# GpSimd's sum jobs in the three cycles around the exchange of the resident operands

## The chip, the cores and the metric

The kernel runs on one core of one Trainium2 chip. The metric is the device time of one execution in microseconds (us), lower is better. TensorE (PE) multiplies, VectorE (DVE) and ScalarE (ACT) work on tiles in SBUF and PSUM, GpSimd (POOL) too, and DMAs move data between HBM and SBUF. DMAs are issued from three queues here: SyncE's (SP), ScalarE's and GpSimd's.

## The reference, cut to what matters

One layer: RMSNorm, a chunked spatial-gating mixer, a residual add, RMSNorm, a squared-ReLU MLP, a residual add and the final RMSNorm. The change lies in how the MLP is computed.

```python
def channel_mlp(h, w1, w2):
    a = jax.nn.relu(h @ w1)
    return (a * a) @ w2
# h: 2048 x 1024, w1: 1024 x 4096, w2: 4096 x 1024, float32
x = x + mixer_chunked_sgu(rmsnorm(x, norm_mix_g[i]), ...)
x = x + channel_mlp(rmsnorm(x, norm_mlp_g[i]), mlp_w1[i], mlp_w2[i])
return rmsnorm(x, final_g)
```

## The kernel before, in words

**Precision.** Every float32 operand of TensorE is split into a rounded part and a rest: ScalarE writes the `_hi` copy (`u_hi`, `x_hi`, `a_hi`, `d_hi`), VectorE subtracts it from the raw tile and writes `_lo`. Each product is three matmuls (hi x hi, hi x lo, lo x hi).

**Stages.** First the mixer, in four blocks of 512 tokens (`BLOCKS` = 4), until about 577 us. Then the MLP by a 2 x 2 block scheme that needs seven products where eight would be usual, but needs sums and differences of blocks as operands. The up stage (h times w1) has `UP` = 16 cycles of `STEPS` = 7 steps, `SECOND` = 112 steps in all; a step is 24 matmuls of 512 columns. The down stage (times w2) has 8 cycles of 7 steps of 48 matmuls. TensorE runs through both in order (line 1263).

**The resident operands.** In the up stage the seven token operands `x_raw[0..6]` of 1 MB each stay in SBUF for eight cycles (`UP // PAIRS` = 8), and the weights `u_raw` (512 KB a step, four slots) stream past them. Steps 0 to 55 work on the first pair of token blocks, steps 56 to 111 on the second. The exchange is written out by hand. When step 49 + i has ended, operand i is free, and ScalarE's queue issues the load of its successor (`up_operand(act, 1, i)`, line 302). ScalarE and VectorE split it in step 52 + i (`renew`, lines 581 and 849), and TensorE needs it in step 56 + i. So the loads of 7 MB are issued from the end of step 49 on, and the splits go on to step 58.

**The order on each engine.** Instructions of an engine run in the order of the program. In step g, ScalarE and VectorE first split the weight of step g + 2 (`ahead`: lines 571 and 838), then take or finish results, then split a resident operand (`renew`). ScalarE copies products out of the PSUM banks (`keep_bank`, line 755); step g needs the banks of step g - 2. VectorE makes the operands of the down stage from the results (`finish_second`, lines 1017 to 1029), in two halves, in the third and fourth step of the next cycle. ScalarE's copy in that fourth step overwrites what `finish_second` reads, and so waits for it.

**GpSimd's jobs.** The weight sums are made by `add_up(n)`, 40 jobs in the order of `jobs`. A job waits until the job before it is stored, loads 1 MB into the one tile `job`, makes four dependent 128 x 512 `tensor_tensor` operations on it (lines 491 to 497, both inputs in SBUF), and stores 1 MB (`w1sum`, `xs` or `w2sum`, line 507). Twenty jobs are done in the mixer stage. In the up stage `next_jobs` is called once a cycle, after `pool.wait_ge(products, step_done(u * STEPS))`, which is the end of the first step of cycle u: two jobs in cycles 0 and 1, one in each later cycle, but none in cycles 6, 7 and 8. What is left is done in the down stage, after four accumulating DMAs onto `Y` (line 542). The sums `w2sum` of chunk 2 are needed before the 17th step of the down stage and those of chunk 3 before its 24th.

Counted from the code: jobs 24 to 27 run in cycles 2 to 5, jobs 28 to 34 in cycles 9 to 15, jobs 35 to 39 in the down stage.

Of the kernel before, what the change touches and what calls it, by code (L numbers as in the profile page):

```python
# [31 lines left out]
def build(nc: bass.Bass, x, xT, gains_T, final_g, a_w_in, a_w_s, a_b_s, a_w_out,  # L32
          mlp_w1, mlp_w2, out):
    _, L, D = x.shape
    F = mlp_w2.shape[1]
    G = a_w_s.shape[1]
# [4 lines left out]
    PAIRS = BLOCKS // 2  # L41
# [10 lines left out]
    UP = PAIRS * CHUNKS * 2  # L52
# [106 lines left out]
    with ExitStack() as ctx:  # L159
# [78 lines left out]
        def step_done(g, j=None):  # L238

            j = width(g) - 1 if j is None else j  # L240
            return 4 * FIRST + (2 * g if g < SECOND else 4 * g - 2 * SECOND) + j + 1
# [210 lines left out]
        def _(pool):  # L452
# [63 lines left out]
            def next_jobs(count):  # L516
                nonlocal n
                for _ in range(count):
                    if n < len(jobs):
                        add_up(n)  # L520
                        n += 1
# [8 lines left out]

            for u in range(UP):
                pool.wait_ge(products, step_done(u * STEPS))
                if not UP // PAIRS - 2 <= u <= UP // PAIRS:
                    next_jobs(2 if u < 2 else 1)


            for half, cols, i in FIRST_PARTS:
# [767 lines left out]
```

## Time and profile before

| what | value |
|---|---|
| time, median of 3 runs | 1824.14 us (1823.81 to 1824.42) |
| the profiled execution | 1827.29 us |
| span of the profile (first to last instruction) | 1825.5 us |
| granted TensorE clock, mean | 0.996 |
| busy: TensorE, VectorE, ScalarE, GpSimd | 1802.2, 1111.1, 782.5, 407.1 us |
| moved by DMA | 445.40 MB, mean 244 GB/s |

The span is given from the first instruction, and all positions in the trace count from there. A busy TensorE is one with matmuls in flight; "idle before" is the time in which an engine had none, with what ended it. The granted clock 1.00 is 2.4 GHz and 0.50 is 1.2 GHz.

### The profile page before, as it was taken

The page shows a single profiled execution, that of the slowest core. Times are in us where ns is not written, and L with a number is a line of the kernel's source. Part 1 is how long each engine was busy: PE and PEld are TensorE (multiplying, and loading weights), DVE is VectorE, ACT ScalarE, POOL GpSimd, SP SyncE. Part 2 cuts the span into 40 slices and gives each one's busy share as a digit, 9 for nine tenths or more (in the row PEclk, how much of TensorE's full clock was granted, in tenths as well). Part 3 has the DMA queues.
Part 4 walks back from the last instruction along what each step waited for, and adds up shares of the span by engine and source line. Part 5 has one row for each costly group of instructions (what it writes and reads, how often), then busy time and mean ns, then how long its engine had stood idle before and what let it go on. Part 6 is the DMA issues. An engine that isn't in the chain of part 4 may idle for free.

```text
span 1825.5 us, 20165 instructions
## 1 busy us (share of the span) xinstructions
PE 1802.2 (99%) x8136; PEld 1497.9 (82%) x8136; DVE 1111.1 (61%) x1122; ACT 782.5 (43%) x880; POOL 407.1 (22%) x394
## 2 busy tenths in 40 slices
PE   9999999999999899999999999999999999999998
PEld 7888888888888788888878888878888888888886
DVE  3583483484384566654666655685666666866665
ACT  5553544434534533444543443354433335333333
POOL 2442442432340133310002111110234002000002
PEclk9999999999999899999999999999999999999999
DMA  8757656665655588875957777799977555854552
GB/s 329 269 209 267 240 215 241 244 244 204 234 199 201 199 290 267 303 263 183 355 197 237 259 256 229 278 367 319 309 299 264 220 202 201 288 184 185 199 205 103
DMA packets 134157, 445.40 MB, mean 244 GB/s; under 512 B 8112, under 2 KB 9136, under 8 KB 118320
## 3 DMA queue, kind: packets, MB, share of 16 engines
q1 hardware_dynamic: 105728, 329.02, 51.3%
q0 software_dynamic: 25168, 92.80, 14.3%
q10 hardware_dynamic: 3168, 22.30, 3.2%
q8 instruction: 64, 1.05, 0.2%
q14 instruction: 29, 0.24, 0.0%
HBM read 318.26 MB, written 125.83 MB: 243 GB/s over the span
## 4 chain that ended last, share of the span: by engine, by line
PE 92%; DVE 2%; DMA 2%; ACT 1%; SPq 1%; issue 1%; DVEq 0%; POOLq 0%; POOL 0%; ACTq 0%
PE bank L1263 62%; PE bank L1098 28%; DMA u_raw<-in_mlp_w 1%; PE bank L1144 1%; PE bank L1120 1%; SPq L312 1%; DMA bias_rows<-in_a_b_s 1%; PE bank L1147 0%; DMA x_raw<-xs 0%; DVE Y L1036 0%; ACT x_hi L581 0%; DVE x_lo L849 0%; DVE r L1017 0%; DVE sums L1020 0%; DVE u_lo L838 0%
## 5 line engine op out<-in xcount | busy, mean ns | idle before, releaser
L1263 PE MATMUL bank<-x_hi,u_hi 128*128 128x512 f32 x896 | 351.0, 392 | 8.0 <-ACT c L755 4.8
L1263 PE MATMUL bank<-x_lo,u_hi 128*128 128x512 f32 x896 | 349.9, 391 | 0.0
L1263 PE MATMUL bank<-x_hi,u_lo 128*128 128x512 f32 x896 | 349.8, 390 | 0.0
L1263 PE MATMUL bank<-d_lo,a_hi 128*128 128x512 f32 x896 | 348.9, 389 | 0.0
L1263 PE MATMUL bank<-d_hi,a_hi 128*128 128x512 f32 x896 | 348.9, 389 | 0.0
L1263 PE MATMUL bank<-d_hi,a_lo 128*128 128x512 f32 x896 | 348.9, 389 | 0.0
L838 DVE TENSOR_TENSOR u_lo<-u_raw,u_hi 128x1024 fp32r<-128x1024 f32 x112 | 148.9, 1329 | 180.2 <-ACT u_hi L571 180.2
L1007 DVE TENSOR_TENSOR Y<-bank,Y 128x512 f32<-128x512 f32 x208 | 138.0, 686 | 179.8 <-PE bank L1263 179.6
L576 ACT ACTIVATE d_hi<-d_raw 128x2048 fp32r<-128x2048 f32 x56 | 107.4, 1919 | 282.2 <-DMA d_raw<-w2sum 153.7
L832 DVE TENSOR_TENSOR w_lo<-w_raw,w_hi 128x2048 fp32r<-128x2048 f32 x47 | 116.5, 2490 | 171.5 <-ACT w_hi L566 160.5
L1263 PEld LDWEIGHTS bank<-x_hi,u_hi 128*128 128x128 f32 x896 | 168.9, 189 | 45.6 <-issue 8.4
L1263 PEld LDWEIGHTS bank<-x_hi,u_lo 128*128 128x128 f32 x896 | 168.9, 189 | 35.3
L1263 PEld LDWEIGHTS bank<-x_lo,u_hi 128*128 128x128 f32 x896 | 169.0, 189 | 34.6
L1263 PEld LDWEIGHTS bank<-d_hi,a_lo 128*128 128x128 f32 x896 | 168.3, 188 | 34.8
L1263 PEld LDWEIGHTS bank<-d_hi,a_hi 128*128 128x128 f32 x896 | 168.3, 188 | 34.8
L1263 PEld LDWEIGHTS bank<-d_lo,a_hi 128*128 128x128 f32 x896 | 168.3, 188 | 34.8
L571 ACT ACTIVATE u_hi<-u_raw 128x1024 fp32r<-128x1024 f32 x112 | 117.1, 1057 | 136.9 <-DMA u_raw<-in_mlp_w 63.4
L755 ACT ACTIVATE c<-bank 128x512 f32<-128x512 f32 x96 | 55.5, 596 | 216.7 <-DVE sums L1029 112.2
L844 DVE TENSOR_TENSOR d_lo<-d_raw,d_hi 128x2048 fp32r<-128x2048 f32 x56 | 128.9, 2302 | 23.1 <-ACT d_hi L576 23.1
L855 DVE TENSOR_TENSOR a_lo<-a_raw,a_hi 128x2048 fp32r<-128x2048 f32 x56 | 132.3, 2363 | 6.2 <-ACT a_hi L585 6.2
L585 ACT ACTIVATE a_hi<-a_raw 128x2048 fp32r<-128x2048 f32 x56 | 107.4, 1917 | 49.8 <-DMA a_raw<-a2s 49.8
L491 POOL TENSOR_TENSOR job<-job 128x512 f32<-128x512 f32 x32 | 55.6, 1737 | 240.3 <-DMA job<-in_mlp_w 240.3
(113 smaller groups left out, 2763.3 us busy)
## 6 DMA issues: line engine op xcount, KB each, us to landing
a_raw<-a2s SPq DMA_DIRECT2D x56, 1024.0 KB, 7.3
a2s<-sums SPq DMA_DIRECT2D x32, 1280.0 KB, 7.9
job<-in_mlp_w POOLq DMA_DIRECT2D x32, 1024.0 KB, 8.2
u_raw<-w1sum SPq DMA_DIRECT2D x64, 512.0 KB, 4.7
d_raw<-w2sum SPq DMA_DIRECT2D x32, 1024.0 KB, 4.9
w_raw<-in_a_w_in SPq DMA_DIRECT2D x31, 1024.0 KB, 5.9
u_raw<-in_mlp_w SPq DMA_DIRECT2D x48, 512.0 KB, 5.4
d_raw<-in_mlp_w SPq DMA_DIRECT2D x24, 1024.0 KB, 5.2
```

The costliest lines, as they stand in the source:

```text
L491: pool.tensor_tensor(q3, q3, q1, ALU.subtract).then_inc(job_step, 1)
L571: act.activation(u_hi[g % SLOTS][:, :, :], u_raw[g % SLOTS][:, :, :], ACT.Copy)\
L576: act.activation(d_hi[d % SLOTS][:, :, :], d_raw[d % SLOTS][:, :, :], ACT.Copy)\
L585: act.activation(a_hi[d % SLOTS][:, :, :], a_raw[d % SLOTS][:, :, :], ACT.Copy)\
L755: act.activation(to, bank_of(g, j)[:, :], func).then_inc(act_read, 1)
L832: dve.tensor_tensor(w_lo[s][:, :, :], w_raw[s][:, :, :], f32(w_hi[s][:, :, :]), ALU.subtract)\
L838: dve.tensor_tensor(u_lo[s][:, :, :], u_raw[s][:, :, :], f32(u_hi[s][:, :, :]), ALU.subtract)\
L844: dve.tensor_tensor(d_lo[s][:, :, :], d_raw[s][:, :, :], f32(d_hi[s][:, :, :]), ALU.subtract)\
L855: dve.tensor_tensor(a_lo[s][:, :, :], a_raw[s][:, :, :], f32(a_hi[s][:, :, :]), ALU.subtract)\
L1007: dve.tensor_tensor(rows, bank_of(g, j)[:, :], rows, ALU.add).then_inc(dve_read, 1)
L1098: ins = pe.matmul(banks[j][:, :], stationary(x_part, k, j), moving(y_part, k, j), start=first and k == 0 and n == 0, stop=final and k == K ...
L1263: ins = pe.matmul(bank_of(g, j)[:, :], stationary[x_part][:, k, j * P:(j + 1) * P], moving[y_part][:, k, :], start=i in (0, 1, 3) and k == ...
```

## The change

GpSimd calls `next_jobs` in every cycle of the up stage, in 6, 7 and 8 too. Nothing else is edited. Since the jobs are numbered through, job 28 runs in cycle 6, 29 in cycle 7, 30 in cycle 8, and each later cycle has the job that stood three cycles behind it. Cycle 15 ends with job 37, and jobs 38 and 39 stay for the down stage.

```diff
             for u in range(UP):
                 pool.wait_ge(products, step_done(u * STEPS))
-                if not UP // PAIRS - 2 <= u <= UP // PAIRS:
-                    next_jobs(2 if u < 2 else 1)
+                next_jobs(2 if u < 2 else 1)
```

## Rows read from the trace of the kernel before

**Rows 1.** The page: busy time by engine, and the chain's shares by engine.
```profile
PE 1802.2 (99%) x8136; PEld 1497.9 (82%) x8136; DVE 1111.1 (61%) x1122; ACT 782.5 (43%) x880; POOL 407.1 (22%) x394
...
PE 92%; DVE 2%; DMA 2%; ACT 1%; SPq 1%; issue 1%; DVEq 0%; POOLq 0%; POOL 0%; ACTq 0%
```

**Rows 2.** Windows: stretch, length, busy PE PEld DVE ACT POOL, clock, DMA share, GB/s.
```profile
787.00:825.00 38.00, 38.00 (x169) 31.50 (x168) 23.89 (x25) 15.47 (x23) 7.70 (x6) 1.00 0.73 250
825.00:863.00 38.00, 38.00 (x169) 31.47 (x169) 19.93 (x25) 15.70 (x23) 0.00 (x0) 1.00 0.61 193
863.00:901.00 38.00, 37.48 (x166) 30.77 (x165) 25.12 (x27) 16.76 (x19) 0.00 (x0) 1.00 0.92 331
901.00:939.00 38.00, 34.53 (x152) 27.99 (x151) 28.29 (x29) 24.05 (x32) 0.00 (x0) 1.00 0.63 212
...
1167.00:1205.00 38.00, 36.48 (x161) 29.62 (x160) 23.00 (x23) 16.41 (x20) 7.79 (x6) 1.00 0.93 347
...
1282.00:1358.00 76.00, 76.00 (x337) 62.96 (x337) 51.95 (x42) 30.81 (x20) 19.30 (x15) 1.00 0.86 305
```

**Rows 3.** Timeline of GpSimd: start, length, instruction, idle before and its end.
```profile
788.79 0.71 POOL L481 DMA_DIRECT2D job<-in_mlp_w  x1 [15.59 <-PE bank L1263]
...
946.29 0.71 POOL L481 DMA_DIRECT2D job<-in_mlp_w  x1 [141.35 <-PE bank L1263]
955.72 1.54 POOL L491 TENSOR_TENSOR job<-job 128x512 f32<-128x512 f32 x1 [8.71 <-DMA job<-in_mlp_w]
...
1174.39 0.71 POOL L481 DMA_DIRECT2D job<-in_mlp_w  x1 [21.94 <-PE bank L1263]
1186.16 1.29 POOL L491 TENSOR_TENSOR job<-job 128x512 f32<-128x512 f32 x1 [11.06 <-DMA job<-in_mlp_w]
...
1309.72 3.32 POOL L491 TENSOR_TENSOR job<-job 128x512 f32<-128x512 f32 x1 [21.72 <-DMA job<-in_mlp_w]
```

**Rows 4.** Timeline of ScalarE and its queue in the exchange.
```profile
864.75 0.33 ACTq L302 DMA_DIRECT2D x_raw<-xs  x1
...
879.05 1.06 ACT L571 ACTIVATE u_hi<-u_raw 128x1024 fp32r<-128x1024 f32 x1 [2.89 <-DMA u_raw<-in_mlp_w]
885.26 0.60 ACT L755 ACTIVATE c<-bank 128x512 f32<-128x512 f32 x1 [5.15 <-DVE sums L1029]
...
897.49 1.06 ACT L571 ACTIVATE u_hi<-u_raw 128x1024 fp32r<-128x1024 f32 x1 [3.84 <-DMA u_raw<-in_mlp_w]
...
928.28 1.08 ACT L755 ACTIVATE c<-bank 128x512 f32<-128x512 f32 x2 [10.16 <-DVE sums L1029]
```

**Rows 5.** Timeline of VectorE, in the exchange and in cycle 15.
```profile
905.51 2.29 DVE L849 TENSOR_TENSOR x_lo<-x_raw,x_hi 128x2048 fp32r<-128x2048 f32 x1 [4.83 <-ACT x_hi L581]
...
923.17 1.22 DVE L838 TENSOR_TENSOR u_lo<-u_raw,u_hi 128x1024 fp32r<-128x1024 f32 x1
...
927.55 0.69 DVE L1029 TENSOR_TENSOR sums<-sums 128x512 f32<-128x512 f32 x1
...
1187.73 2.18 DVE L838 TENSOR_TENSOR u_lo<-u_raw,u_hi 128x1024 fp32r<-128x1024 f32 x1 [2.41 <-ACT u_hi L571]
1189.83 1.77 DVE L1017 TENSOR_TENSOR r<-r 128x512 f32<-128x512 f32 x1
```

**Rows 6.** The chain that ended last, in order of time: start, length, what.
```profile
886.44 11.03 DMA u_raw<-in_mlp_w
...
929.02 250.52 PE bank L1263 x1104
```

**Rows 7.** Windows in the exchange, columns as in Rows 2.
```profile
878.00:892.00 14.00, 13.85 (x62) 11.13 (x60) 8.83 (x10) 7.80 (x8) 0.00 (x0) 1.00 0.99 353
892.00:906.00 14.00, 13.64 (x60) 11.36 (x61) 9.17 (x9) 10.16 (x14) 0.00 (x0) 1.00 1.02 373
```

**Rows 8.** Windows after a stop of TensorE of 4.4 us, and around one of 3.4 us.
```profile
616.00:622.00 6.00, 6.00 (x24) 5.18 (x24) 1.19 (x2) 3.48 (x5) 0.00 (x0) 0.67 0.50 201
920.00:935.00 15.00, 11.59 (x51) 9.31 (x50) 12.47 (x16) 4.33 (x6) 0.00 (x0) 1.00 0.45 158
```

## The prediction

> **What bounds the kernel now.** Read the page first: TensorE is busy 99% of the span and makes 92% of the chain that ended last [rows 1]. So a change off TensorE can gain only where TensorE stands idle, and costs only where it makes a new idle stretch. Next, look at each cycle in the windows. In an up cycle with a job (787 to 825 us) TensorE is busy 38.00 of 38.00 us, in one without (825 to 863) too [rows 2]. The idle time sits in the exchange: 38.00 - 37.48 = 0.5 us in cycle 7, then 38.00 - 34.53 = 3.5 us in cycle 8, and 38.00 - 36.48 = 1.5 us in cycle 15, where the down operands are loaded [rows 2]. The down stage, 1282 to 1358, shows 76.00 of 76.00 [rows 2].
>
> The third view is the chain in order of time, read backwards from TensorE's restart at 929.02 [rows 6]. ScalarE's bank copy at 928.28 had waited 10.16 us for VectorE's `sums` of line 1029, begun at 927.55 [rows 4, 5]. VectorE's 22 instructions from 905.51 to that point follow each other without a gap over 0.3 us, and before the first it had waited 4.83 us for ScalarE's `x_hi` [rows 5]. ScalarE in turn had waited 3.84 us until 897.49 for a weight, and that load was issued at 886.44 and took 11.03 us [rows 4, 6]. So the stop of 3.5 us has two parents: a weight that lands late in a stretch whose DMA share is 0.99 to 1.02 [rows 7], and then some 23 us of VectorE work without a pause. Neither contains a GpSimd job: it is idle for 141.35 us before 946.29 [rows 3]. The change puts jobs into both.
>
> **What moves.** Three jobs move from the down stage into cycles 6, 7 and 8; per job 1 MB is loaded, four operations are made, 1 MB is stored. The count of instructions is the same.
>
> Removed from the down stage: 3 MB of loads, 3 MB of stores, 12 GpSimd operations. I cost this at nothing, because TensorE had no idle time where they stood [rows 2]. Had that cover not been there, the most that these jobs take from VectorE would be the amount worked out below, about 4 us each. What comes next there is the accumulating DMAs and jobs 38 and 39, which now end earlier; jobs 31 to 37 run in the same slots as 28 to 34 did, with other addresses. Nothing is late that was in time.
>
> Added in cycle 6: the job's turn comes one cycle after the window that began at 788.79 plus 38, so near 827 us, and with 9.4 us from issue to the first operation, as from 946.29 to 955.72 [rows 3], some 7 us of operations and a store as long as the load it is over by about 853. DMA share is 0.61 there, against 0.73 with a job in the cycle before, and the exchange begins at 864.75 [rows 2, 4]. TensorE was fully busy in the same phase with a job. Cost 0.
>
> Added in cycle 7: GpSimd waits for step 49, the very step that frees the first operand, so its load is issued at about 865, together with the first of the seven operand loads [rows 4]. Cycle 15 is the twin of this moment: a job's load issued at 1174.39 next to the first operand loads of the down stage had its first operation 11.8 us after the issue, where 9.4 is seen in a quiet cycle [rows 3]. I take 12 us: the four operations stand at about 877 to 884. VectorE's chain there starts with the weight that landed at 879.05 and ends with `finish_second`, for which the bank copy at 885.26 waited [rows 4]. In the twin the same operations grew: 2.18 us where the split of a weight takes 1.22 without a job, and 1.77 where a short operation takes 0.69 [rows 5], about 1 us for each GpSimd operation met. Two or three are met, so 2 to 3 us; with 1 to 2 us for the weight itself (1 MB more at 353 GB/s is 3.0 us if it all stands ahead, 0 if none does [rows 7]) the bank copy comes 3 to 5 us later. TensorE needed that bank when step 53 ended, which is when the weight load of 886.44 was issued [rows 6], so a new stop of some 3.5 us appears at step 54. It does not add to the later one in full: ScalarE has 3.84 us of waiting at 893.65 to 897.49 and VectorE 4.83 us before 905.51 [rows 4, 5], and these take up a shift of up to about 4 us. TensorE loses the same time earlier, not twice.
>
> What does reach the end is the delay of the 886.44 load itself. The job's store, issued at about 884 to 885, runs beside it: 1 MB at 353 to 373 GB/s [rows 7] is 2.8 to 3.0 us. Bounds 0 (TensorE's new stop postpones the competing operand loads) and 3.0; a single load shared with one more stream is neither, so I take the middle, **1.4 us**.
>
> Added in cycle 8: GpSimd waits for step 56. It ended near 904 (946.29 is seven steps later: minus 38 minus 3.5 us of stop), in the new kernel near 907. First operation 9.4 us behind the issue [rows 3], all four at about 916 to 923, in the middle of VectorE's unbroken stretch that sets TensorE's restart. The price of four such operations beside dense VectorE work is a pair of rows: 23.89 us of VectorE time in a cycle with a job, 19.93 in one without, both with 25 instructions, so 3.96 us [rows 2]. In the twin, where VectorE had gaps, the three operations that met it grew by about 3.1 us (0.96 + 1.08 + 1.08, of which two rows stand) [rows 5]. The stretch here has no gap, so I take **3.9 us**; bounds 0 (the operations miss the stretch) and 4.4 (1.1 us each).
>
> For this I weigh a rule. The rows show a VectorE operation with both inputs in SBUF growing by 1 us, not by GpSimd's whole 1.3 to 1.5 us [rows 2, 3, 5]. The Trainium skill (SBUF — State Buffer, section Who interferes with whom) says that such an operation and a GpSimd one that reads SBUF exclude each other for the whole instruction. By that rule, taken to the letter, 4 x 1.29 = 5.2 us would be lost, not 3.9, and the forecast would be 1.3 us later. It speaks against this change in either form; the trace agrees with the sign and puts the size lower.
>
> TensorE's clock: after a stop of 4.4 us it was granted 0.67 on average over 6 us, that is partly the 1.2 GHz level; around the 3.5 us stop it stayed at 1.00 [rows 8]. If a stop now reaches 4.4 us at the end, 6 x (1 - 0.67) = 2 us more are lost. Split into two stops, each may stay under; I take 0, bound 2.0.
>
> **Sum.** 0 + 0 + 1.4 + 3.9 + 0 = +5.3 us, against the profiled execution's own 1827.29: 1832.6. That execution lies 3.15 us above the median of the plain runs; on the median 1824.14 the same sum gives **1829.4 us**. The lowest sum with the VectorE term in the middle of the stretch is +3.1, the highest 3.0 + 4.4 + 2.0 = +9.4.
>
> **The rivals.** Measurement can tell about 0.2%, or 3.6 us.
>
> (a) Hidden, not slower: the cycle 8 job misses VectorE's stretch. It would have to land after 928, that is take 20 us and more; one load did wait 21.72 us, beside accumulating DMAs [rows 3]. Against it: those DMAs are absent, and the last operand load is issued after step 55, some 33 us behind 864.75 [rows 4]. Equally the waits of 3.84 and 4.83 us may take up more than I grant them. Then 0 to 3.0 us remain, 1824.1 to 1827.1, about 1825.5. The point from which it decides is whether GpSimd's operations start before about 925. Chance 0.20.
>
> (b) The loads pile up: the exchange is already at full DMA share for 28 us [rows 7], and load and store of the cycle 7 job both go ahead of the 886.44 weight: 2 x 3.0 + 3.9 + 2.0 for the clock = 11.9, so 1836. Against it: work that waits less urgently, the operands themselves, can give way. Chance 0.07.
>
> (c) Faster: the last sums leave the down stage, where one job waited 21.72 us for its load [rows 3]. If the slow loads there cost TensorE time, it would be gained. The windows show none [rows 2], so this is worth at most a fraction of a microsecond unless the plain runs differ from the profiled one; 1820 would need idle time that is not there. Chance 0.03.
>
> The forecast has 0.70. Of it about 0.06 lies under +3.6 us. So slower by over 0.2%: 0.64 + 0.07 = 0.71; within: 0.20 + 0.06 = 0.26; faster 0.03. The range runs from +1.1 (inside rival a) to +9.4: 1825.2 to 1833.5.
>
> **What would show it.** In the profile of the changed kernel: GpSimd operations at about 877 to 884 and 916 to 923; short VectorE operations of 1.7 us there instead of 0.69; a stop of TensorE before step 54 (near 887 to 890) and one before step 61 that ends near 934; the weight of 886.44 landing at 897.5 to 900.5; the down stage unchanged at full occupation. The forecast is wrong if VectorE has gaps between 907 and 930, if the cycle 8 operations start after 925, or if the weight lands far later than 900.5.

## The result

| | median, us | profiled execution, us |
|---|---|---|
| before | 1824.14 (1823.19 to 1824.42, 5 runs) | 1827.29 |
| changed | 1832.79 (1832.41 to 1832.91, 5 runs) | 1832.79 |

The ratio is 1.005, with a 95% interval of 1.0038 to 1.0061: the change costs 8.65 us by the medians, 7 to 11 by the interval. One of the ten executions of only8_late, a kernel of the experiments, took 5369 us for a reason that no trace shows, and is in no comparison.

The page of the changed kernel, as in [rows 1], and rows picked from two views, the chain in order of time and GpSimd's timeline (start, length, what):

```profile
PE 1803.2 (98%) x8136; PEld 1498.2 (82%) x8136; DVE 1113.0 (61%) x1122; ACT 782.5 (43%) x880; POOL 399.6 (22%) x394
...
PE 92%; DMA 3%; DVE 2%; SPq 1%; issue 1%; ACT 1%; DVEq 0%; POOLq 0%; POOL 0%
```
```profile
865.47 10.81 DMA u_raw<-in_mlp_w
884.40 12.78 PE bank L1262 x48
897.19 13.75 DMA u_raw<-w1sum
916.65 2.32 DVE u_lo L837
933.01 251.94 PE bank L1262 x1104
```
```profile
860.31 0.71 POOL L481 DMA_DIRECT2D job<-in_mlp_w  x1 [21.93 <-PE bank L1262]
873.57 1.28 POOL L491 TENSOR_TENSOR job<-job 128x512 f32<-128x512 f32 x1 [12.55 <-DMA job<-in_mlp_w]
...
902.91 0.71 POOL L481 DMA_DIRECT2D job<-in_mlp_w  x1 [22.06 <-PE bank L1262]
913.31 1.28 POOL L491 TENSOR_TENSOR job<-job 128x512 f32<-128x512 f32 x1 [9.69 <-DMA job<-in_mlp_w]
914.66 3.24 POOL L493 TENSOR_TENSOR job<-job 128x512 f32<-128x512 f32 x1
```

The shares of the page hardly move, so the windows have to be read. Columns are those of [rows 2]:

```profile
825.00:863.00 38.00, 38.00 (x169) 31.47 (x168) 23.81 (x26) 15.47 (x23) 7.78 (x6) 1.00 0.73 251
863.00:901.00 38.00, 35.36 (x149) 28.79 (x148) 24.88 (x26) 18.54 (x23) 6.74 (x5) 0.96 0.99 382
901.00:939.00 38.00, 29.64 (x124) 23.84 (x123) 29.91 (x27) 16.88 (x18) 9.73 (x6) 0.91 0.68 236
...
1282.00:1358.00 76.00, 76.00 (x337) 62.94 (x336) 48.95 (x39) 32.75 (x20) 17.03 (x14) 1.00 0.88 299
```

Cycle 6 with its job keeps TensorE fully busy, and so does the down stage. The idle time of the two windows of the exchange is 2.6 and 8.4 us, where it was 0.5 and 3.5 [rows 2], and matmuls are missing for a second reason: the clock's mean falls to 0.96 and 0.91. TensorE's restarts (idle before in brackets):

```profile
884.40 0.47 PE L1262 MATMUL bank<-x_hi,u_hi 128*128 128x512 f32 x1 [2.64 <-ACT c L754]
933.01 0.77 PE L1262 MATMUL bank<-x_hi,u_hi 128*128 128x512 f32 x1 [7.81 <-ACT c L754]
```

To compare kernels I count from the first operand load, which is issued when step 49 ends. In the changed kernel it is this row, against 864.75 before [rows 4]:

```profile
860.10 0.33 ACTq L302 DMA_DIRECT2D x_raw<-xs  x1
```

TensorE's restart before step 61 lies 933.01 - 860.10 = 72.9 us behind it; before it was 929.02 - 864.75 = 64.3 [rows 4, 6]. That is +8.6 us. Then the clock:

```profile
933.00:940.00 7.00, 6.99 (x25) 5.70 (x26) 4.16 (x5) 4.61 (x7) 0.00 (x0) 0.79 0.01 2
```

Behind the restart 7 us were granted 0.79 on average, part of them at 1.2 GHz, so 7 x 0.21 = 1.5 us of matmul time went, where the clock had stayed at 1.00 around the stop before [rows 8]. In these two profiled executions the exchange is thus 10.1 us longer. The medians differ by less, 8.65 us, probably because the clock can fall behind the unchanged stop too, as the experiments show (0.59 to 0.78); it did not in the execution shown ahead.

### The profile page after: what moved, and what is told of

Same layout as the page of the kernel before. It is cut to its first block, busy times and chain, and to the rows that moved or that the text cites. A ratio compares the mean times of both kernels' runs of the same rounds, so it can differ in the third digit from the quotient of the medians.

```text
span 1831.0 us, 20167 instructions
## 1 busy us (share of the span) xinstructions
PE 1803.2 (98%) x8136; PEld 1498.2 (82%) x8136; DVE 1113.0 (61%) x1122; ACT 782.5 (43%) x880; POOL 399.6 (22%) x394
## 4 chain that ended last, share of the span: by engine, by line
PE 92%; DMA 3%; DVE 2%; SPq 1%; issue 1%; ACT 1%; DVEq 0%; POOLq 0%; POOL 0%
PE bank L1262 62%; PE bank L1097 27%; PE bank L1143 1%; DMA u_raw<-in_mlp_w 1%; PE bank L1119 1%; DMA u_raw<-w1sum 1%; SPq L312 1%; DMA bias_rows<-in_a_b_s 1%; PE bank L1146 0%; DVE Y L1035 0%; DVE r L1016 0%; DMA x_raw<-xs 0%; DVE sums L1019 0%; DVE u_lo L837 0%; SPq L328 0%
## 5 line engine op out<-in xcount | busy, mean ns | idle before, releaser
L854 DVE TENSOR_TENSOR a_lo<-a_raw,a_hi 128x2048 fp32r<-128x2048 f32 x56 | 127.9, 2285 | 6.3 <-ACT a_hi L584 6.3
L565 ACT ACTIVATE w_hi<-w_raw 128x2048 fp32r<-128x2048 f32 x47 | 89.5, 1909 | 41.8 <-DMA w_raw<-in_a_w_out 21.7
```

Source lines behind the costliest of these rows:

```text
L565: act.activation(w_hi[w % SLOTS][:, :, :], w_raw[w % SLOTS][:, :, :], ACT.Copy)\
L854: dve.tensor_tensor(a_lo[s][:, :, :], a_raw[s][:, :, :], f32(a_hi[s][:, :, :]), ALU.subtract)\
```

## The experiments

All ratios are against runs of the kernel before on the same chip, with 95% intervals; 0.001 is 1.8 us. "Restart" is TensorE's restart before step 61, counted from the first operand load; "stop" its idle time there; "clock" the mean grant over the 7 us behind the restart, from windows like the one above. These three come from one profiled execution of each kernel. The ratios rest on 4 (ops_only) to 12 (writes_only) executions of the kernel named. The kernels dma_only, ops_only, ops8_only and writes_only leave out or alter some of the weight sums, so their results are wrong and only their times count.

| kernel | ratio | restart, us | stop, us | clock |
|---|---|---|---|---|
| before | 1 | 64.3 | 3.41 | 1.00 |
| changed | 1.0050 (1.0038 to 1.0061) | 72.9 | 7.81 | 0.79 |
| only6 | 1.0006 (0.9997 to 1.0016) | 66.4 | 3.41 | 0.59 |
| only7 | 1.0013 (1.0002 to 1.0025) | 67.9 | 3.7 | 0.76 |
| only8 | 1.0028 (1.0016 to 1.0040) | 67.3 | 6.59 | 0.60 |
| only8_late | 1.0006 (0.9996 to 1.0015) | 64.4 | 3.42 | 0.76 |
| dma_only | 1.0020 (1.0010 to 1.0030) | 67.6 | 3.98 | 0.76 |
| ops_only | 1.0051 (1.0036 to 1.0066) | 70.0 | 5.89 | 0.60 |
| ops8_only | 1.0036 (1.0023 to 1.0048) | 68.0 | 6.58 | 0.75 |
| writes_only | 1.0016 (1.0005 to 1.0027) | 63.4 | 3.41 | 0.78 |
| order_after | 1.0034 (1.0022 to 1.0047) | 70.3 | 5.99 | 0.61 |
| pause7_8_15 | 0.9988 (0.9979 to 0.9997) | 63.3 | 2.17 | 1.00 |
| order_before | 0.9979 (0.9971 to 0.9988) | 61.9 | 0.54 | 1.00 |
| order_pause | 0.9969 (0.9958 to 0.9979) | 60.8 | 0.92 | 1.00 |

### Which of the three jobs costs

```diff
-                next_jobs(2 if u < 2 else 1)
+                if u not in (7, 8):      # only6;  only7: (6, 8);  only8: (6, 7)
+                    next_jobs(2 if u < 2 else 1)
```

> Pause in cycles 7 and 8 only, so job 28 runs in cycle 6 and nothing runs in the exchange. Theory A (the price is paid where a job meets the exchange): same as the kernel before, +0.0, bounds -0.5 to +0.7 us; the stop before step 61 stays at about 3.5 us. Rival B (what costs is that jobs come earlier or that the down stage has fewer of them): a third of the loss, about +3 us.

Measured 1.0006, +1.1 us (-0.5 to 2.9), an interval that includes 1. The 3 us of rival B (a third of the loss for each) lie at its upper end. The cycle 6 job costs nothing that can be told.

The profile of only6 also shows how far single executions scatter. GpSimd is idle for 108 us before 946.33 there, and yet the restart is 2.1 us later than before: the weight load issued at 881.64 took 13.17 us, where its counterpart took 11.03 [rows 6], and TensorE stood idle for 2.43 us before 906.34. So a difference of some 2 us in the restart of two single executions proves nothing.

> Pause in cycles 6 and 8, so one job runs in cycle 7, beside the first operand loads. Theory A: a new stop of about 3 us before step 54, taken up again by ScalarE's and VectorE's waiting; at the end +1 to +3 us, through a weight that lands later. Rival C (two jobs are needed to make the queue of loads too long, one is absorbed): +0 to +0.7 us. Rival B: +3 us.

Measured 1.0013, +2.4 us (0.4 to 4.6), which excludes 0 narrowly, and does not by itself separate the rivals (C up to 0.7, B 3) from theory A. The new stop before step 54 is there, 2.52 us. From the chain of this kernel:

```profile
865.63 11.41 DMA u_raw<-in_mlp_w
...
884.43 12.80 PE bank L1263 x48
897.25 12.15 DMA u_raw<-w1sum
```

The weight that comes late is the one issued after step 55 (897.25, for step 59), not the one of step 53 on which the prediction looked.

> Pause in cycles 6 and 7, so one job runs in cycle 8, whose four operations fall into VectorE's unbroken stretch. Theory A: VectorE's operations there grow by 3.3 us and the stop before step 61 with them; with 0 to 2 us for its load and 1.4 us where TensorE's clock falls to 0.50 after the longer stop, +4 to +6 us. Rival C (the operations cost little, it is the loads): +0 to +2 us.

Measured 1.0028, +5.1 us (2.9 to 7.3), inside theory A's band, and rival C (0 to 2) falls. VectorE's timeline, columns as in [rows 5]:

```profile
913.95 2.32 DVE L838 TENSOR_TENSOR u_lo<-u_raw,u_hi 128x1024 fp32r<-128x1024 f32 x1
916.20 1.79 DVE L1017 TENSOR_TENSOR r<-r 128x512 f32<-128x512 f32 x1
917.91 1.77 DVE L1020 SCALAR_TENSOR_TENSOR sums<-c 128x512 f32<-128x512 f32 x1
919.60 1.77 DVE L1023 TENSOR_TENSOR sums<-sums,r 128x512 f32<-128x512 f32 x1
```

These four operations grew by about 1.1 us each; the next is back at 0.68. TensorE's stop went from 3.41 to 6.59 us:

```profile
931.40 0.77 PE L1263 MATMUL bank<-x_hi,u_hi 128*128 128x512 f32 x1 [6.59 <-ACT c L755]
```

### The same job five steps later

```diff
-                next_jobs(2 if u < 2 else 1)
+                if u == 8:
+                    pool.wait_ge(products, step_done(61))
+                if u not in (6, 7):
+                    next_jobs(2 if u < 2 else 1)
```

> Pause in cycles 6 and 7; the job of cycle 8 waits for the end of step 61 in place of step 56, so that it falls behind VectorE's stretch and the exchange. Theory A (it is the place that costs): same as before, 0 to +1 us, against +5.1 us for the same job five steps earlier. Rival B (a further job in the up stage costs wherever it stands): about +5 us.

Measured 1.0006, +1.1 us (-0.7 to 2.7), so rival B's 5 us fall; the stop is again 3.42 us. It is the place that costs, not the job.

### Transfers and operations apart

```diff
+                if n in (29, 30):        # dma_only: one column in place of 512
+                    for i in range(4):
+                        pool.tensor_tensor(job[:, i, 0:1], job[:, i, 0:1], job[:, i, 1:2], ALU.subtract)
+                        ...              # the semaphore steps as in the other jobs
```

> All three jobs at their places, but the jobs of cycles 7 and 8 make their four operations on one column only, so those 2 MB of sums hold other values: their transfers stay, their load on SBUF goes. Theory A (in the changed kernel the stretch from step 49 to step 63 is 10.1 us longer: 5.3 us by weights that land late, 3.3 by VectorE's operations grown beside GpSimd's, 1.4 by TensorE's clock): about +5 us against the kernel before, +4 to +6.5, with VectorE's short operations at 0.69 us throughout. Rival D (GpSimd's operations are nearly all of it): +0 to +2 us.

Measured 1.0020, +3.6 us (1.8 to 5.5), between theory A's band (4 to 6.5) and rival D's (0 to 2), and clear of zero: the transfers do cost. VectorE's short operations were 0.69 us, and the chain is that of only7: a load of 11.37 us issued at 865.99, a stop of 2.06 us before step 54, and the weight issued after step 55 (897.09) late again, with 12.44 us.

```diff
+                load(29)                 # in cycle 6; ops_only
+                for m, step in ((29, step_done(52, 0)), (30, step_done(58))):
+                    pool.wait_ge(products, step)
+                    ... the four operations of job m on the same tile
+                pool.wait_ge(products, step_done(62))
+                store(29); load(30); store(30)
```

> Three jobs, but of those of cycles 7 and 8 the load comes before the exchange, the operations of both stand in the middle of step 52 and after step 58, and the store, a load and a store come after step 62; the second set works on the first's data, so those sums hold other values. No job transfer lies in the exchange, the operations do. Theory A: +3.3 us by VectorE's growth before step 61, and up to 1.5 us more by the clock: +3 to +5 us. Rival E (the transfers are all of it, the growth is hidden): +0 to +1 us.

Measured 1.0051, +9.3 us (6.6 to 12.0): over both theories, and as much as the whole change, though only four executions stand behind it. The restart explains 70.0 - 64.3 = 5.7 of it, the clock 7 x 0.40 = 2.8 more. VectorE's timeline has both groups:

```profile
874.48 2.00 DVE L867 TENSOR_TENSOR u_lo<-u_raw,u_hi 128x1024 fp32r<-128x1024 f32 x1 [3.22 <-ACT u_hi L600]
876.41 1.78 DVE L1046 TENSOR_TENSOR r<-r 128x512 f32<-128x512 f32 x1
878.11 1.78 DVE L1049 SCALAR_TENSOR_TENSOR sums<-c 128x512 f32<-128x512 f32 x1
...
912.82 1.79 DVE L1046 TENSOR_TENSOR r<-r 128x512 f32<-128x512 f32 x1
914.54 1.78 DVE L1049 SCALAR_TENSOR_TENSOR sums<-c 128x512 f32<-128x512 f32 x1
916.24 1.77 DVE L1052 TENSOR_TENSOR sums<-sums,r 128x512 f32<-128x512 f32 x1
917.94 1.78 DVE L1054 TENSOR_TENSOR sums<-r,sums 128x512 f32<-128x512 f32 x1
```

The second group adds 4 x 1.09 = 4.4 us to the stretch that sets the restart. The first adds 3 us early, of which 1.3 to 1.4 seem left at 5.7 - 4.4; that is within the scatter of single executions seen in only6. Theory A had left out such a carry, and put the clock too low. A further 0.76 us is a stop before 1008.98, outside the exchange: the jobs displaced behind step 62 come in quick succession there, and the four operations of one, from 998.37 on, meet VectorE's next `finish_second`. To separate the groups, the first was moved behind step 58 and the second behind step 62:

```diff
-                for m, step in ((29, step_done(52, 0)), (30, step_done(58))):
+                for m, step in ((29, step_done(58)), (30, step_done(62))):
```

> As ops_only, but the first set of four operations stands after step 58 and the second after step 62, behind the exchange: no job transfer in the exchange and one set in VectorE's stretch. Revised theory F (ops_only restarted TensorE 5.8 us later than the kernel before: 4.4 by the four short operations grown in the stretch, 1.4 carried over from the stop before step 54; then 2.8 by the clock): the 1.4 go, so VectorE's second finish ends 4.4 us later and the kernel is 4.4 to 7.5 us slower than before. If the first set was the cause, under +2 us.

Measured 1.0036, +6.6 us (4.2 to 8.8), inside the expected band; under 2 us, as for the first set as the cause, is excluded. Four operations in the stretch and no job transfer near it give about what job 30 alone gave (only8, 5.1): the cycle 8 job costs by its operations. The two intervals (2.9 to 7.3 and 4.2 to 8.8) overlap, so its transfer may still be worth up to about 3 us.

### What of GpSimd's work blocks VectorE

```diff
-                        pool.tensor_tensor(to, a, b, ALU.add if i == 2 else ALU.subtract).then_inc(job_step, 1)
+                        pool.memset(job[:, :, :], float(i)).then_inc(job_step, 1)
```

> ops_only with each operation replaced by a memset of the whole tile, so GpSimd writes SBUF and reads none of it; those sums hold constants. Theory F with the shared read interface as the cause: VectorE's operations stay at 0.69 us, the stop before step 61 is that of the kernel before, and the time is +0 to +1.5 us (the jobs displaced into the later cycles stay displaced). Rival G (any GpSimd work on SBUF blocks VectorE): growth by about 1 us an operation as in ops_only, +8 to +9 us.

GpSimd was as busy at the same places, but VectorE's operations did not grow there:

```profile
909.24 7.44 POOL L542 MEMSET job<- 128x2048 f32 x4 [28.14 <-PE bank L1292]
```
```profile
911.50 0.69 DVE L1046 TENSOR_TENSOR r<-r 128x512 f32<-128x512 f32 x1
912.10 0.69 DVE L1049 SCALAR_TENSOR_TENSOR sums<-c 128x512 f32<-128x512 f32 x1
912.70 0.69 DVE L1052 TENSOR_TENSOR sums<-sums,r 128x512 f32<-128x512 f32 x1
```

The stop is 3.41 us again, and rival G falls. The time, +2.9 us (0.9 to 4.9), is above the expected 0 to 1.5. The profile shows two parts of it: the clock behind the stop (7 x 0.22 = 1.5 us), and a stop of 0.72 us before 1002.00 like that of ops_only. There a displaced job's `tensor_tensor` operations, from 991.00 on, met VectorE's `finish_second`, and three VectorE operations grew by 1.1 us each. No run tests these displaced jobs alone. Against ops_only, which differs only in the eight operations themselves (the memsets also write the whole tile each), it is about 6 us faster. The Trainium skill (SBUF — State Buffer, section Who interferes with whom) says that a VectorE instruction with two SBUF inputs contends with a GpSimd one that reads SBUF and not with one that only writes; these two runs agree, 1.78 us against 0.69.

### Which work on VectorE sets the restart, and a faster kernel

In step 58 VectorE splits the last operand, which TensorE needs only in step 62, ahead of the second half of `finish_second`, for which the restart waits. The edit exchanges the two:

```diff
                 if c and i in (2, 3):
                     finish_second(c - 1, i - 2)
-                renew(g)
+                second = UP // PAIRS * STEPS
+                if g == second + 3:
+                    renew(g - 1)
+                if g != second + 2:
+                    renew(g)
```

> The changed kernel, with the split of the last operand moved behind finish_second's second half on VectorE. If VectorE's stretch sets the restart in the changed kernel, as in the one before: 2.3 us faster than the changed kernel and up to 1.5 more by the clock, so +4.5 to +6.5 us against the kernel before. If the late weight alone sets it, +8.6 us.

Measured 1.0034, +6.2 us (4.0 to 8.6), so 2.9 us better than the changed kernel by the two central ratios, inside the expected band; the two intervals overlap, though, and the 8.6 us of the rival are the end of this one. The restart is 2.6 us earlier. The clock gave part of it back: 0.61 in place of 0.79.

> The kernel before, with that one move and its own pause in cycles 6, 7 and 8. The same kernel with the pause in 7, 8 and 15 ran 5.6 us faster than before, of which the pause alone gave 2.2: so 3.4 us faster, -2.3 to -4.

The kernel that this expectation quotes is order_pause, which ran before it and stands below. Measured 0.9979, -3.8 us (-5.3 to -2.2); the stop shrinks from 3.41 to 0.54 us, with the clock at 1.00.

> Pause in cycles 7, 8 and 15, a job in every other cycle, so that cycle 15, where the down operands are loaded, has none either. By theory A the stop of 1.5 us in cycle 15 belongs to VectorE's operations grown by 3.1 us beside the job of that cycle: it goes, and the kernel is 1 to 1.5 us faster than before. By the rival that the stop is the down operands' own, 0.

Measured 0.9988, -2.2 us (-3.8 to -0.5), so the rival's 0 lies just outside. In cycle 15 the stop of 1.5 us [rows 2] is gone. Of this kernel, columns of [rows 2]:

```profile
1167.00:1205.00 38.00, 38.00 (x169) 31.49 (x168) 23.24 (x27) 19.61 (x24) 0.00 (x0) 1.00 0.90 314
```

> The kernel with the pause in cycles 7, 8 and 15, and on VectorE the split of the last operand (2.28 us) moved from before finish_second's second half to behind it. If VectorE's stretch sets the stop before step 61, that stop gets 2.2 us shorter and the kernel is about 4 us faster than before (2.2 us of which the pause alone gave). If something else ends last there, no more than the pause's 2.2 us.

Measured 0.9969, -5.7 us (-7.7 to -3.8): within the intervals, the two gains add up. This kernel is faster than both, and it does the opposite of the change: it widens the pause by cycle 15, and only cycle 6 is taken out of it.

## Why the prediction was right, and where it was not

**Right.** The sign and the range (1825.2 to 1833.5 against 1832.79). Cycle 6 costs nothing that can be told (only6). The jobs removed from the down stage bring 0: its windows are full in both. The first stop appears before step 54, at 884.40, 2.64 us where some 3.5 were expected. VectorE's stretch sets the restart and GpSimd's operations stand in it, from 913.31 on; that is 53.2 us behind the first operand load, where the expected 916 is 51.3. Rival (a), hidden, failed at its own point: the operations started well before 925. Rival (c) found no idle time to win.

**The VectorE term, 3.9 us.** In the changed kernel four operations met the stretch and three grew in full:

```profile
914.40 2.33 DVE L848 TENSOR_TENSOR x_lo<-x_raw,x_hi 128x2048 fp32r<-128x2048 f32 x1
916.65 2.32 DVE L837 TENSOR_TENSOR u_lo<-u_raw,u_hi 128x1024 fp32r<-128x1024 f32 x1
918.90 1.77 DVE L1016 TENSOR_TENSOR r<-r 128x512 f32<-128x512 f32 x1
920.60 1.78 DVE L1019 SCALAR_TENSOR_TENSOR sums<-c 128x512 f32<-128x512 f32 x1
```

1.10 + 1.08 + 1.09 = 3.3 us. At the first of the four VectorE lost next to nothing (2.33 for 2.28); there it was GpSimd's operation of 914.66 that took 3.24 us, where most take 1.3 to 1.6. The mechanism and the bounds held. In only8 and ops8_only it was 4.4. Neither came to the 5.2 us of mutual exclusion over whole instructions.

**The transfer term, 1.4 us: the failed step.** It was put on the weight issued at 886.44. In the changed kernel that load was issued at 881.79 and ScalarE split it at 892.16 without waiting. The late one was two steps on, the weight of step 59, and ScalarE did wait for it:

```profile
910.97 1.06 ACT L570 ACTIVATE u_hi<-u_raw 128x1024 fp32r<-128x1024 f32 x1 [4.97 <-DMA u_raw<-w1sum]
912.06 1.23 DVE L837 TENSOR_TENSOR u_lo<-u_raw,u_hi 128x1024 fp32r<-128x1024 f32 x1 [3.74 <-ACT u_hi L570]
```

The same weight before, its issue and VectorE's split of it:

```profile
898.09 5.76 SPq L337 DMA_DIRECT2D u_raw<-w1sum  x2
911.44 1.22 DVE L838 TENSOR_TENSOR u_lo<-u_raw,u_hi 128x1024 fp32r<-128x1024 f32 x1
```

VectorE's split began 912.06 - 860.10 = 52.0 us behind the first operand load, and 911.44 - 864.75 = 46.7 us behind it before. So this term measured 5.3 us, not 1.4, and went beyond its own bound of 3.0. Two things made the weight late. It was issued 37.1 us behind the first operand load (897.19), where it had been 33.3, since its load waits for the end of step 55 and TensorE had lost time before that: 2.64 us by the new stop (a stop of 0.52 us in this stretch before is gone), and about 1.6 us by the clock behind it:

```profile
884.00:888.00 4.00, 3.60 (x9) 2.86 (x10) 1.43 (x1) 4.00 (x5) 0.00 (x0) 0.60 1.04 373
```

Then it took 13.75 us, where it had taken 8.4. Together that is 9.1 us, of which the engines' waiting took up 3.8. So the prediction was right that about 4 us can be taken up, but not that nothing of the first stop comes through: it followed one weight, and not TensorE's lateness into the issue of the next ones. It said that the new stop postpones the competing operand loads, counted that as relief, and did not follow where they went. The last three came 24.1, 31.7 and 38.6 us behind the first, onto the weights of steps 58 and 59 (issued at 31.7 and 37.1); before, it was 21.7, 27.1 and 37.2.

It is the job of cycle 7 that does it. In the four profiled kernels with its transfers (changed, only7, dma_only, order_after) VectorE's split of this weight began 50.0 to 52.0 us behind the first operand load, in the ten others 45.3 to 48.8. One of those ten is ops_only: it has the same first stop, 2.56 us, and the same late issue, 37.0 us, but without the transfers the load landed after 9.6 us and the split began at 48.1. So the late issue alone does not give the 5.3 us; the long load is needed too. How much of the long load is the job's store, and how much the bunched operand loads, no run separates.

**The clock, 0 with a bound of 2.0.** It fell behind both stops of the changed kernel. It cost about 1.6 us behind the first, which is part of the 5.3 above, and 1.5 behind the second; in the experiments with a stop of 5.9 to 6.6 us it cost 1.7 to 2.8. The hope "split into two stops, each may stay under" failed: the second was 7.81 us, and the first brought the clock down at 2.64.

**The sum.** By these terms 5.3 + 3.3 + 1.5 = 10.1 us in the profiled pair, against 5.3 predicted and +9.4 as the highest sum. The median, 8.65, is inside the range and 3.4 us above the forecast. That the range held is in part luck: one term was over its bound, and what kept the sum inside was a VectorE term at its low side and a median of the kernel before that, probably, already holds some clock losses.

Transfers and operations do not add up in the central values (3.6 and 9.3 alone, 8.65 together), though their intervals would just allow it; in the restart they nearly do, 67.6 - 64.3 = 3.3 and 5.7 against 8.6 together. The clock is one thing that does not add. In the changed kernel the second half of the long stop, 929 to 933, was already granted about 0.5, so that part of the low grant fell where TensorE stood idle. Behind the restart it cost 1.7, 2.8 and 1.5 us. And 0.76 us of ops_only lie outside the exchange.

## What to carry to other kernels

A gap in a helper engine's work can be what keeps a critical stretch short: before filling it, find the engine whose unbroken work ends the next stop, and ask whether the helper reads SBUF beside its two-input operations. When a new stop postpones transfers, follow each one to where it now falls. The same reading pays in the other direction: moving one 2.3 us operation behind what is waited for gave 3.8 us (2.2 to 5.3), while moving the pause to cycle 15 gave 2.2.

## What the runs showed of the hardware

- A GpSimd operation that reads SBUF cost a VectorE operation with two SBUF inputs about 1.1 us (0.69 to 1.78) in most meetings; in one, at 914.40 of the changed kernel, VectorE kept its 2.33 us and GpSimd's operation took 3.24. GpSimd memsets of a similar total length (7.4 us for four) cost VectorE nothing (0.69).
- The stop of 3.41 or 3.42 us before step 61 is the same in four executions (before, only6, only8_late, writes_only), and the clock behind it was 1.00, 0.59, 0.76 and 0.78. After stops of 0.54, 0.92 and 2.17 us there it was 1.00, but after the first stops of 2.06 us (dma_only) and 2.64 us (changed) it was 0.57 and 0.60 over 884 to 888. So the same stop can cost nothing or 2.9 us, and one profile doesn't tell which.
- The entry to the up stage varies in the same way. Before, the windows from 592 and from 616 us were both granted less; in the changed kernel, whose code is the same there, they were granted 1.00. First the row of before, then those of the changed kernel:

```profile
592.00:602.00 10.00, 7.97 (x29) 6.10 (x28) 10.00 (x10) 6.03 (x7) 0.00 (x0) 0.83 0.67 279
...
592.00:602.00 10.00, 7.98 (x41) 6.43 (x40) 10.00 (x10) 6.66 (x9) 0.00 (x0) 1.00 0.66 273
602.00:616.00 14.00, 10.68 (x52) 9.22 (x51) 8.53 (x7) 9.22 (x11) 0.00 (x0) 0.88 0.61 224
616.00:622.00 6.00, 6.00 (x28) 4.97 (x27) 1.98 (x3) 4.62 (x8) 0.68 (x1) 1.00 0.49 191
```

The last window was granted 0.67 before [rows 8]. The first operand load comes 4.65 us earlier (860.10 against 864.75), which is why positions are counted from it and why spans of single executions (1825.5 and 1831.0, 5.5 us apart) do not measure the change.
